# Two-block transformer kernel: down biases in one transfer over 96 partitions, the router's modulation units dealt to other places, and another order inside the first expert

## The chip, the cores and the metric

One core of a Trainium2 chip runs the whole program in one launch. The metric is the device time of an execution in microseconds (us), and the median of several executions is compared. All values are float32; the weights are read from HBM, some 585 MB in an execution.

## What is computed

Two transformer blocks run one after the other on 256 tokens of width 1024. The first has a mixer, cross attention and a mixture of experts; the second has two attention layers and two MLPs, whose modulation (`ada`) is a product of one vector with large matrices. The part that matters here is the mixture of experts (MoE):

```python
logits = (hf @ w_router) + b_router               # 256 tokens, 32 experts
top_v, top_i = lax.top_k(logits, 4)
top_w = jax.nn.softmax(top_v, axis=-1)
...
def expert_block(args):                           # for each expert e and its tokens xb
    xb, e = args
    gu = xb @ w_gate_up[e] + b_gate_up[e]         # 1024 -> 2048
    gate = jnp.minimum(gu[:, :D_EXPERT], SWIGLU_LIMIT)
    up = jnp.clip(gu[:, D_EXPERT:], -SWIGLU_LIMIT, SWIGLU_LIMIT)
    glu = gate * jax.nn.sigmoid(SWIGLU_ALPHA * gate)
    return ((up + 1.0) * glu) @ w_down[e] + b_down[e]
...
m = jax.nn.silu(c) @ w + b                        # the second block's modulation ("ada")
```

## The kernel before

The program is written engine by engine, each engine's instructions in the order in which they stand in the code, with semaphores between them. TensorE (PE) multiplies, ScalarE (ACT) and VectorE (DVE) work on what it leaves in the PSUM banks, GpSimd (POOL) does little, and SyncE (SP) issues nearly all DMAs on one queue.

**Weights in granules.** SP brings the weights in pieces of 2 MB, the granules, into eight slots of SBUF (`ring`). `PRE` is the list of granules used ahead of the experts, `FILL_ORDER` the order in which SP issues them. `SLOTS` slots are reused: a fill waits until PE has used the granule that had the slot before (semaphore `granules_used`, in the code `used`, which counts granules in the order of their use). Four granules of the modulation, `SIDE`, lie outside the ring, in free parts of `arena` and `XN`. An expert has six granules: four of `w_gate_up` (j = 0 to 3) and two of `w_down`. For the first expert these are called q0 to q5 here, and q6, q7 are the first two of the second expert. `AHEAD` says behind which granule of the modulation SP issues q0 to q5. q6 and q7 take the two ring slots in which the last two ring units of the modulation lay, so their fills wait for the use of those.

**The router's three units.** PE multiplies the modulation vector with twelve units of `ada` weights, (`ada(n)`: the next n units; line 1406). Units 9, 10 and 11 are used in the router's stage: unit 9 behind the transposes of the normalised tokens, unit 10 behind the router's logits, unit 11 behind the positions of the tokens. Before the change unit 9 is the side unit (in `arena[0:4096]`) and units 10 and 11 lie in the ring. The gate and up bias rows `bias_gu_r` are written by ACT (line 992) over a part of the same `arena` region, so ACT waits for the use of the side unit first. Behind them ACT copies the last group of the modulation (`ada_copy`, line 887) and the down biases into `dn_r` (line 996); DVE then makes the low parts (lines 2539 and 2545).

**Down biases.** `b_down` (32 experts x 1024) is wanted three times, one below the other, in 96 partitions of `dn_raw`. SP issues it between q4 and q5, in three transfers of 32 partitions.

**Small transfers at the start.** ACT issues thirteen DMAs on its own queue before it computes: six vectors of 8 rows of 512 B (`norm_mem`, `norm_mix`, `norm_xattn`, `norm_ffn`, `c_2`, `norm_final`), two of 4 rows, one of 2, one of 12, two of 24 and one of 96, 214 rows together.

**The first expert.** PE gathers its tokens (`gather`, line 1581), sends the overflow count and the transposed gates (lines 1602 and 1605; DVE makes tables and `gatT_r` from them), and waits for the gathered tokens `xe`, which DVE scales (line 2494, semaphore `e_xe`). Then come the bias rows (`bias_gu`, line 1627), four times `gate_up` (line 1635), between them `ada_combine` (line 1418), `extra_table` (lines 1612 to 1614), `down_bias` (line 1622), then the hidden layer's transposes (line 1647) and `down` (line 1654). The other 31 experts have the same form, without the tables, and with `scatter` (line 1665).

Of the kernel before, what the change touches and what calls it, by code (L numbers as in the profile page):

```python
# [19 lines left out]
F32 = mybir.dt.float32  # L20
# [7 lines left out]
P = 128  # L28
S = 256
TB = S // P  # L30
D = 1024
KC = D // P
NE = 32
# [3 lines left out]
NCAND = (NB_MAX - 1) * NE  # L37
NX_MAX = S * TOPK // CAP
SLOT = 4096
# [81 lines left out]
PRE = pre_stream()  # L121
# [4 lines left out]
SLOTS = 8  # L126
R0 = 4
R1 = 8
SIDE = {PRE.index(("ada", u)): SLOTS + i for i, u in enumerate((4, 5, 8, 9))}
SIDE_FILL = {4: 32, 5: 48, 8: 80, 9: 96}  # L130
RING = [g for g in range(NPRE) if g not in SIDE]
NR = len(RING)
assert PRE[RING[NR - R0]] == ("w_o", 0)
E_SLOTS = [7, 6, (NR - R0) % R0, (NR - R0 + 1) % R0, 4, 5] + [(NR - R0 + j) % R0 for j in range(2, R0)]
E_BLOCK = 4
HEAD = [("w_k", 0), ("w_k", 1)]
TAIL = [("w_o", 0), ("w_o", 1), ("ada", 8), ("ada", 10), ("ada", 11), ("ada", 9)]
FILL_ORDER = ([PRE.index(p) for p in HEAD] + [g for g in range(NPRE) if PRE[g] not in HEAD + TAIL]
              + [PRE.index(p) for p in TAIL])
assert len(set(FILL_ORDER)) == NPRE  # L140
AHEAD = {("ada", 8): (0,), ("ada", 11): (1,), ("ada", 9): (2, 3, 4, 5)}
SPLIT = [p for p in PRE if p[0] != "ada"]
PER_E = 6
MOE_END = NPRE + NE * PER_E
# [94 lines left out]
def build_program(nc, A, tab_d, dft_d, out_d):  # L239
    ctx = ExitStack()  # L240
    with ctx:
        sems = {}

        def sem(name):
            if name not in sems:
                sems[name] = ctx.enter_context(nc.semaphore(name))
            return sems[name]

        def done(name, i):

            if (name, i) in PRE:
                return sem("granules_used"), USED_AT[PRE.index((name, i))]
            return sem("granules_used"), MOE_END + POST.index((name, i)) + 1
# [25 lines left out]
        B = [ctx.enter_context(nc.psum_tensor(f"bank{i}", [P, HW], F32)) for i in range(8)]  # L279
# [24 lines left out]
        flag = stat[0:NCAND, 56:57]  # L304
# [6 lines left out]
        ident, tri, ones, quads, iota = (tb_(n) for n in ("ident", "tri", "ones", "quads", "iota"))  # L311
        eps5, eps6, zero = tb_("eps5"), tb_("eps6"), tb_("zero")

        def slot(s, w=SLOT):
            assert s < SLOTS
            return ring[:, s * SLOT:s * SLOT + w]

        def arn(a, w):
            return arena[:, a:a + w]
# [39 lines left out]
        dn_raw = arn(5120, D)[0:3 * NE]  # L359
        dn_r = XT_rf[0:3 * NE, 0:D]  # L360
        gatT_r = XT_rf[0:3 * NE, D:D + TB * P].rearrange("p (t n) -> p t n", t=TB)
        gat3_r = XT_rf[:, D + TB * P:D + TB * P + TB * 96].rearrange("p (t a e) -> p t a e", t=TB, a=3)
# [80 lines left out]
        def unit_parts(u):  # L443

            if u == 8:
                places = [XNf, arn(6144, 2048)]
            elif u in SIDE_FILL:
                places = [{4: slot(SLOTS - 1), 5: arn(2048, SLOT), 9: arn(0, SLOT)}[u]]
            else:
                places = [slot(slot_of(PRE.index(("ada", u))))]  # L450
            k = KC // len(places)
            return [(k * i, x.rearrange("p (k n) -> p k n", k=k)) for i, x in enumerate(places)]
# [148 lines left out]
        def _(sp):  # L601
# [8 lines left out]
            def fill(g, name, i):  # L610
                o = OWNER[g]
                if o is not None and PRE[o] in SPLIT:
                    sp.wait_ge(sem("w_hi"), half_no(PRE[o][0], 2 * PRE[o][1] + 1))
                    sp.wait_ge(sem("w_lo"), half_no(PRE[o][0], 2 * PRE[o][1] + 1))
                elif o is not None:
                    sp.wait_ge(used, USED_AT[o])
                if (name, i) == ("ada", 4):
                    sp.wait_ge(sem("fft_seq"), 4)
                elif (name, i) == ("ada", 5):
                    sp.wait_ge(sem("mix_sum"), 2)  # L620
                    sp.wait_ge(*done("ada", 4))
                elif (name, i) == ("ada", 8):
                    sp.wait_ge(*upto("xa", "sq", 2))
                    sp.wait_ge(*done("ada", 5))
                elif (name, i) == ("ada", 9):
                    sp.wait_ge(sem("xa_o"), 4)
                    sp.wait_ge(*done("ada", 8))
                for dst, src in granule_source(name, i, slot_of(g)):
                    sp.dma_start(dst, src).then_inc(landed[slot_of(g)], 16)
# [8 lines left out]

            def down_bias_fill():

                for r in range(3):
                    sp.dma_start(dn_raw[NE * r:NE * r + NE], A["b_down"][0]).then_inc(sem("bias_landed"), 16)

            def expert_source(j, e):
                if j < 4:
# [9 lines left out]
            for g in FILL_ORDER[2:]:  # L655
                name, i = PRE[g]
# [50 lines left out]
            with sp.If(n > 0):  # L707
                sp.wait_ge(used, MOE_END)
                with sp.Fori(0, n) as i:
                    e = nc.values_load(table_i[0:1, bass.ds(i, 1)], engines=[ENG.SP], min_val=0, max_val=NE - 1)  # L710
# [133 lines left out]
        def _(act):  # L844
# [142 lines left out]
                act.activation(rt[:, t, 0:NE], logit[:, t, 0:NE], ACT.Exp,  # L987
                               bias=att[:, 2, t:t + 1]).then_inc(sem("rt_e"), 1)
            act.wait_ge(sem("bias_landed"), 16 * 8)
            act.wait_ge(*done("ada", 9))  # L990
            for m in range(2):
                act.activation(bias_gu_r[m], bias_raw[m], ACT.Copy).then_inc(sem("bias_hi"), 1)
            ada_copy()
            act.wait_ge(sem("logits"), 1)
            act.wait_ge(sem("bias_landed"), 16 * 11)
            act.activation(dn_r, dn_raw, ACT.Copy).then_inc(sem("bias_hi"), 1)

            def expert(i, down_done):
# [279 lines left out]
        def _(pe):  # L1278
# [132 lines left out]
            def ada_combine():  # L1411

                a, b, _, comb = ADA_GROUPS[group[0]]
                n = b - a
                group[0] += 1
                pe.wait_ge(sem("ada_part"), group[0])
                for c in range(4):
                    mm = pe.matmul(B[comb][:, n * c:n * c + n], ada_part[:, c * P:(c + 1) * P], quads[:, 0:n],
                                   start=True, stop=True)
                mm.then_inc(sem("ada_comb"), 1)  # L1420
# [55 lines left out]
            for i, b in enumerate((6, 7, 2, 3)):  # L1476
                if b == 2:
                    pe.wait_ge(sem("mix_c"), 2)
                for e in range(TB):
                    mm = pe.matmul(B[b][:, e * S:(e + 1) * S], U[:, e, i * P:(i + 1) * P], dft[:, e * S:(e + 1) * S],  # L1480
                                   start=True, stop=True)
# [45 lines left out]
            for m in range(2):  # L1527
                for t in range(TB):
                    mm = pe.matmul(B[3][:, 2 * m + t:2 * m + t + 1], ssum[:, m, t * P:(t + 1) * P], ones[:, 0:1],
                                   start=True, stop=True)  # L1530
# [67 lines left out]
            pe.wait_ge(*upto("ffn", "xn", 2))  # L1598
            pe.wait_ge(sem("e_sel"), 2)
            gather()  # L1600
            pe.wait_ge(sem("overflow"), 1)
            pe.matmul(B[2][0:NCAND, 65:66], tri[0:NCAND, 0:NCAND], flag, start=True, stop=True).then_inc(sem("rt_mm"), 1)
            pe.wait_ge(sem("gat3"), 2)
            for t in range(TB):
                mm = pe.transpose(B[6][0:3 * NE, t * P:(t + 1) * P],
                                  gat3_r[:, t].rearrange("p a e -> p (a e)").bitcast(F32), ident)
            mm.then_inc(sem("rt_mm"), 1)

            def extra_table():

                pe.wait_ge(sem("overflow"), 2)
                pe.matmul(B[2][0:1, 96:112], tb_("cand_e")[0:NCAND, :], chosen, start=True, stop=True)
                pe.matmul(B[2][0:1, 112:128], tb_("cand_q")[0:NCAND, :], chosen, start=True, stop=True)
                pe.matmul(B[2][0:1, 128:129], ones[0:NCAND, 0:1], flag, start=True, stop=True).then_inc(sem("rt_mm"), 1)
# [10 lines left out]
            def bias_gu():  # L1625
                for m in range(2):
                    pe.matmul(B[m][:], selG, bias_gu_r[m], start=True, stop=False, skip_group_check=True)  # L1627
# [41 lines left out]
            def expert(i, n, first=False):  # L1669

                pe.wait_ge(sem("e_selG"), i * E_BLOCK + (n + 1))
                pe.wait_ge(sem("e_xe"), i * E_BLOCK + (n + 1))
                bias_gu()
                for j in range(4):
                    g = NPRE + n * PER_E + j
                    pe.wait_ge(landed[slot_of(g)], i * (16 * E_BLOCK * PER_E // R1) + FILL[g])
                    gate_up(j, slot_of(g)).then_inc(used, 1)
                    if first and j == 0:
                        ada_combine()
                        extra_table()  # L1680
                    elif first and j == 2:
                        down_bias()
                    elif j == 0:
                        pe.wait_ge(sem("e_y"), i * E_BLOCK + (n + 1))
                        pe.wait_ge(sem("e_ylo"), i * E_BLOCK + (n + 1))
                        scatter()
                pe.wait_ge(sem("e_sel"), i * (2 * E_BLOCK) + (2 * n + 4))
                gather(0, KC - 1)
                pe.wait_ge(sem("e_h"), i * E_BLOCK + (n + 1))
                hidden_T()  # L1690
                gather(KC - 1)
                pe.wait_ge(sem("e_wsel"), i * (2 * E_BLOCK) + (2 * n + 2))
                pe.wait_ge(sem("e_clamp"), i * (2 * E_BLOCK) + (2 * n + 2))
                weights_T()
                pe.wait_ge(sem("e_hTe"), i * E_BLOCK + (n + 1))
                if first:
                    pe.wait_ge(sem("table_ready"), 1)
                for j in range(2):
                    g = NPRE + n * PER_E + 4 + j
                    pe.wait_ge(landed[slot_of(g)], i * (16 * E_BLOCK * PER_E // R1) + FILL[g])  # L1700
                    down(j, slot_of(g)).then_inc(used, 1)
                pe.wait_ge(sem("e_wTe"), i * (2 * E_BLOCK) + (2 * n + 2))
# [1296 lines left out]
```

## Time and profile before

| what | value |
|---|---|
| median of three executions | 1796.16 us |
| lowest and highest of the three | 1792.27 and 1941.92 us |
| the profiled execution's own time | 1793.1 us |
| its span, first to last instruction | 1791.3 us |
| share of the span in which PE is busy | 96% |
| mean DMA rate over the span | 328 GB/s |
| granted clock of PE | 0.995 of full speed |

The profile is one execution with a record of every instruction and DMA packet. Its own time stands 1.8 us above its span, and the two lowest times of the three executions are 3.9 us apart; so terms of a microsecond are compared by the profile, not by the times.

### The profile page before, as it was taken

To read this page: it belongs to the slowest core of one execution; us is meant where nothing else is said; L and a number is where in the kernel's file an instruction comes from. 1 tells how busy PE (TensorE), PEld (TensorE's weight loads), DVE (VectorE), ACT (ScalarE), POOL (GpSimd) and SP (SyncE) were. 2 spreads that over 40 slices of the span, in tenths; PEclk is the share of its full clock that TensorE was granted. 3 is DMA by queue.
4 is the path that set the end of the run, shared out by engine and by line. 5 is a ranking of instruction groups with operands and counts; after the bars stand their busy time and mean duration, and the time that the engine had idled before them with its cause. 6 is when DMAs were issued, how large, how long until landed. Compare 5 with 4: busy or idle time off the path is not lost.

```text
span 1791.3 us, 24226 instructions
## 1 busy us (share of the span) xinstructions
PE 1724.1 (96%) x9828; PEld 1083.8 (61%) x9828; DVE 777.9 (43%) x1327; ACT 524.1 (29%) x694; POOL 33.8 (2%) x40
## 2 busy tenths in 40 slices
PE   8999999999999999999999999999999999899997
PEld 7878754443443434343434343375799988689986
DVE  4454442221221212121212121289887779676555
ACT  5353421111111111111101010247544455644442
POOL 0002000000000000000000000000000010000001
PEclk9999999999999999999999999998999999999999
DMA  9757999999999999999999999975387754335550
GB/s 347 285 200 289 371 396 429 428 427 427 428 429 428 429 428 428 429 428 429 428 428 429 428 429 428 421 283 201 118 286 269 278 205 177 124 119 188 187 210 24
DMA packets 97287, 587.54 MB, mean 328 GB/s; under 512 B 7822, under 2 KB 8036, under 8 KB 71620
## 3 DMA queue, kind: packets, MB, share of 16 engines
q1 hardware_dynamic: 95744, 582.28, 80.5%
q10 hardware_dynamic: 1476, 4.30, 0.7%
q8 instruction: 50, 0.82, 0.2%
q14 instruction: 17, 0.14, 0.0%
HBM read 585.51 MB, written 1.05 MB: 327 GB/s over the span
## 4 chain that ended last, share of the span: by engine, by line
PE 73%; DMA 20%; DVE 3%; ACT 3%; issue 1%; SPq 0%; DVEq 0%; ACTq 0%
PE bank L1321 32%; DMA ring<-in_w_gate_up 19%; PE bank L1635 15%; PE bank L1654 9%; PE bank L1581 4%; PE bank L1903 3%; PE bank L1665 1%; PE bank L1949 1%; PE bank L1627 1%; PE bank L1406 1%; ACT arena L1003 1%; PE bank L1647 1%; ACT sb_XN L1122 1%; DMA ring<-in_w_k 1%; PE bank L2160 0%
## 5 line engine op out<-in xcount | busy, mean ns | idle before, releaser
L1635 PE MATMUL bank<-ring,arena 128*64 128x512 f32 x2048 | 462.6, 597 | 29.0 <-DMA ring<-in_w_gate_up 28.8
L1635 PEld LDWEIGHTS bank<-ring,arena 128*64 128x64 f32 x2048 | 137.5, 136 | 320.2 <-issue 255.3
L1654 PE MATMUL bank<-ring,arena 128*64 128x512 f32 x1024 | 226.8, 595 | 3.3
L1321 PE MATMUL bank<-w_hi,arena_r 128*128 128x512 f32 x672 | 217.2, 392 | 0.9 <-DVE arena_r L2791 0.9
L572 DVE TENSOR_TENSOR w_lo<-ring,w_hi 128x4096 fp32r<-128x4096 f32 (+2 forms) x43 | 188.0, 4373 | 27.9 <-ACT w_hi L561 26.3
L2498 DVE TENSOR_SCALAR arena<-bank 128x512 f32<-128x512 f32 x32 | 22.1, 692 | 367.6 <-PE bank L1635 367.6
L1001 ACT ACTIVATE arena<-arena,sb_tab 128x512 f32<-128x512 f32 x32 | 23.1, 722 | 508.8 <-DVE arena L2498 508.8
L561 ACT ACTIVATE w_hi<-ring 128x4096 fp32r<-128x4096 f32 (+2 forms) x43 | 152.4, 3586 | 20.4 <-DMA ring<-in_c_w_in 12.4
L1654 PEld LDWEIGHTS bank<-ring,arena 128*64 128x64 f32 x1024 | 71.7, 137 | 137.8 <-issue 132.3
L1321 PEld LDWEIGHTS bank<-w_hi,arena_r 128*128 128x128 f32 x672 | 126.2, 188 | 29.3 <-issue 1.9
L1581 PEld LDWEIGHTS bank<-arena,sb_XN 128*128 128x128 f32 x1056 | 123.2, 192 | 26.9 <-issue 26.9
L1581 PE MATMUL bank<-arena,sb_XN 128*128 128x64 f32 x1056 | 128.4, 275 | 0.0
L1321 PE MATMUL bank<-XT_r,w_hi 128*128 128x256 f32 x448 | 127.2, 284 | 0.0
L1321 PE MATMUL bank<-arena_r,w_hi 128*128 128x256 f32 x448 | 126.8, 283 | 0.0
L1321 PE MATMUL bank<-XT_r,w_lo 128*128 128x256 f32 x448 | 126.8, 283 | 0.0
L1321 PE MATMUL bank<-w_lo,arena_r 128*128 128x512 f32 x304 | 118.5, 390 | 0.0
L2519 DVE SCALAR_TENSOR_TENSOR arena_r<-bank,sb_att,arena_r 128x512 fp32r<-128x512 f32 x32 | 24.0, 750 | 217.3 <-ACT arena_r L1006 217.3
L1006 ACT ACTIVATE arena_r<-bank,sb_att 128x512 fp32r<-128x512 f32 x32 | 22.0, 688 | 231.0 <-PE bank L1654 231.0
L545 DVE TENSOR_TENSOR half_lo<-ring,half_hi 128x2048 fp32r<-128x2048 f32 x26 | 59.5, 2290 | 67.8 <-ACT half_hi L535 67.8
L1321 PEld LDWEIGHTS bank<-XT_r,w_hi 128*128 128x128 f32 x448 | 86.0, 192 | 0.7 <-issue 0.2
L1321 PEld LDWEIGHTS bank<-arena_r,w_hi 128*128 128x128 f32 x448 | 86.0, 192 | 0.7 <-issue 0.2
L1321 PEld LDWEIGHTS bank<-XT_r,w_lo 128*128 128x128 f32 x448 | 86.0, 192 | 0.0
(427 smaller groups left out, 2187.9 us busy)
## 6 DMA issues: line engine op xcount, KB each, us to landing
ring<-in_w_gate_up SPq DMA_DIRECT2D x128, 2048.0 KB, 32.0
ring<-in_w_down SPq DMA_DIRECT2D x64, 2048.0 KB, 35.3
ring<-in_mlp_w SPq DMA_DIRECT2D x32, 2048.0 KB, 8.7
ring<-in_ada_w SPq DMA_DIRECT2D x15, 2048.0 KB, 13.3
arena<-in_ada_w SPq DMA_DIRECT2D x48, 256.0 KB, 5.5
ring<-in_c_w_in SPq DMA_DIRECT2D x6, 2048.0 KB, 8.2
ring<-in_w_in SPq DMA_DIRECT2D x4, 2048.0 KB, 8.3
ring<-in_w_v SPq DMA_DIRECT2D x2, 2048.0 KB, 24.2
```

The source lines that it names most:

```text
L545: eng.tensor_tensor(lo[:], half_raw(name, h)[1], hi[:].bitcast(F32), ALU.subtract).then_inc(sem("w_lo"), 1)
L561: ins = eng.activation(dst, raw, ACT.Copy) if on_act else eng.tensor_copy(dst, raw)
L572: eng.tensor_tensor(lo[:, 0:w], slot(slot_of(granule_no(name, i)), w), hi[:, 0:w].bitcast(F32), ALU.subtract).then_inc(sem("w_lo"), 1)
L1001: act.activation(sig, gcl, ACT.Sigmoid, bias=zero, scale=1.702).then_inc(sem("e_sig"), 1)
L1006: act.activation(y_hi, B[2][:], ACT.Copy, scale=slot_gate).then_inc(sem("e_y"), 1)
L1321: mm = pe.matmul(out, st[a], mv[b], start=start and a + b == 0, stop=stop and a == 1, skip_group_check=True)
L1581: mm = pe.matmul(B[3][:, k * CAP:(k + 1) * CAP], XN[:, t, k * P:(k + 1) * P], sel_tok[:, t, :], start=(t == 0), stop=(t == 1))
L1635: mm = pe.matmul(B[m][CAP * h:CAP * h + CAP, :], xe[:, 2 * j + kl, :], w[:, kl, m * D + h * HW:m * D + (h + 1) * HW], start=False, stop=(j ...
L1654: mm = pe.matmul(B[2][CAP * h:CAP * h + CAP, :], hT[:, c, CAP * j:CAP * j + CAP], w[:, c, h * HW:(h + 1) * HW], start=(j == 0 and c == 0), ...
L1903: mm = pe.matmul(b, x[:, k, t * P:(t + 1) * P], parts[wa][:, kl, width * c:width * c + width], start=k + xa + wa == 0, stop=False, skip_gr ...
L2498: dve.tensor_scalar(gcl, B[0][:], 7.0, None, ALU.min).then_inc(sem("e_clamp"), 1)
L2519: dve.scalar_tensor_tensor(y_lo, B[2][:], slot_gate, y_hi.bitcast(F32), ALU.mult, ALU.subtract).then_inc(sem("e_ylo"), 1)
```

## The change

Three things are changed. The down biases come in one transfer whose source names `b_down` three times by a step of 0, over 96 partitions. Of the router's three units, 9 and 10 now lie in the ring and 11 is the side unit. In every expert `bias_gu` now stands ahead of the wait for the tokens. In the first expert the overflow count and the gate transposes (`gates_T`) come behind the first granule, and `extra_table` behind the second.

```diff
-SIDE = {PRE.index(("ada", u)): SLOTS + i for i, u in enumerate((4, 5, 8, 9))}
+SIDE = {PRE.index(("ada", u)): SLOTS + i for i, u in enumerate((4, 5, 8, 11))}
-TAIL = [("w_o", 0), ("w_o", 1), ("ada", 8), ("ada", 10), ("ada", 11), ("ada", 9)]
+TAIL = [("w_o", 0), ("w_o", 1), ("ada", 8), ("ada", 9), ("ada", 10), ("ada", 11)]
-AHEAD = {("ada", 8): (0,), ("ada", 11): (1,), ("ada", 9): (2, 3, 4, 5)}
+AHEAD = {("ada", 8): (0,), ("ada", 10): (1,), ("ada", 11): (2, 3, 4, 5)}
...
-                for r in range(3):
-                    sp.dma_start(dn_raw[NE * r:NE * r + NE], A["b_down"][0]).then_inc(sem("bias_landed"), 16)
+                sp.dma_start(dn_raw, A["b_down"][0][None].to_broadcast((3, NE, D))).then_inc(sem("bias_landed"), 16)
...
             act.wait_ge(sem("bias_landed"), 16 * 8)
-            act.wait_ge(*done("ada", 9))
+            act.wait_ge(*done("ada", 11))
             for m in range(2):
                 act.activation(bias_gu_r[m], bias_raw[m], ACT.Copy).then_inc(sem("bias_hi"), 1)
             ada_copy()
             act.wait_ge(sem("logits"), 1)
-            act.wait_ge(sem("bias_landed"), 16 * 11)
+            act.wait_ge(sem("bias_landed"), 16 * 9)
...
-            pe.wait_ge(sem("overflow"), 1)
-            pe.matmul(B[2][0:NCAND, 65:66], tri[0:NCAND, 0:NCAND], flag, start=True, stop=True).then_inc(sem("rt_mm"), 1)
-            pe.wait_ge(sem("gat3"), 2)
-            for t in range(TB):
-                mm = pe.transpose(B[6][0:3 * NE, t * P:(t + 1) * P],
-                                  gat3_r[:, t].rearrange("p a e -> p (a e)").bitcast(F32), ident)
-            mm.then_inc(sem("rt_mm"), 1)
+            def gates_T():
+
+                pe.wait_ge(sem("overflow"), 1)
+                pe.matmul(B[2][0:NCAND, 65:66], tri[0:NCAND, 0:NCAND], flag, start=True, stop=True).then_inc(sem("rt_mm"), 1)
+                pe.wait_ge(sem("gat3"), 2)
+                for t in range(TB):
+                    mm = pe.transpose(B[6][0:3 * NE, t * P:(t + 1) * P],
+                                      gat3_r[:, t].rearrange("p a e -> p (a e)").bitcast(F32), ident)
+                mm.then_inc(sem("rt_mm"), 1)
...
                 pe.wait_ge(sem("e_selG"), i * E_BLOCK + (n + 1))
+                bias_gu()
                 pe.wait_ge(sem("e_xe"), i * E_BLOCK + (n + 1))
-                bias_gu()
...
                     if first and j == 0:
+                        gates_T()
                         ada_combine()
+                    elif first and j == 1:
                         extra_table()
```

On PE, between the logits and the positions of the tokens, the units stand like this before (`slot0` and `slot1` are ring slots, `arena` the side place):

```order
L1406 MATMUL bank<-ring,sb_cs 32x512 [waits slot0_landed]
L1406 MATMUL bank<-ring,sb_cs 32x512 x7
L1312 MATMUL bank<-sb_tab 128x128 x2
L1591 MATMUL bank<-sb_rt,sb_tab 128x32 [waits rt_mask]
L1592 MATMUL bank<-sb_rt,sb_tab 128x32
L1593 MATMUL bank<-sb_rt,sb_tab 128x32
L1595 MATMUL bank<-sb_tab,sb_vec 96x1 x2
L1406 MATMUL bank<-ring,sb_cs 32x512 [waits slot1_landed]
```

and like this in the changed kernel:

```order
L1405 MATMUL bank<-ring,sb_cs 32x512 [waits slot1_landed]
L1405 MATMUL bank<-ring,sb_cs 32x512 x7
L1311 MATMUL bank<-sb_tab 128x128 x2
L1590 MATMUL bank<-sb_rt,sb_tab 128x32 [waits rt_mask]
L1591 MATMUL bank<-sb_rt,sb_tab 128x32
L1592 MATMUL bank<-sb_rt,sb_tab 128x32
L1594 MATMUL bank<-sb_tab,sb_vec 96x1 x2
L1405 MATMUL bank<-arena,sb_cs 32x512 [waits arena_landed]
```

The ring slots are used by units 9 and 10 in place of 10 and 11, and the side place by the last unit in place of the first.

On PE, from the gather of the first expert's tokens to its second granule (`slot7` has q0, `slot6` has q1), before:

```order
L1581 MATMUL bank<-arena,sb_XN 128x64 x15
L1602 MATMUL bank<-sb_stat,sb_tab 96x1 [waits overflow]
L1605 MATMUL bank<-sb_tab,XT_r 96x128 [waits gat3]
L1605 MATMUL bank<-sb_tab,XT_r 96x128
L1627 MATMUL bank<-arena_r 128x512 [waits e_selG,e_xe,bias_lo,ada_part]
L1627 MATMUL bank<-arena_r 128x512
L1635 MATMUL bank<-ring,arena 64x512 [waits slot7_landed]
L1635 MATMUL bank<-ring,arena 64x512 x7
L1418 MATMUL bank<-sb_tab,arena 128x3 [waits ada_part]
L1418 MATMUL bank<-sb_tab,arena 128x3 x3
L1612 MATMUL bank<-sb_stat,sb_tab 1x16 [waits overflow]
```

and in the changed kernel:

```order
L1580 MATMUL bank<-arena,sb_XN 128x64 x15
L1629 MATMUL bank<-arena_r 128x512 [waits e_selG,bias_lo,ada_part]
L1629 MATMUL bank<-arena_r 128x512
L1637 MATMUL bank<-ring,arena 64x512 [waits slot7_landed,e_xe]
L1637 MATMUL bank<-ring,arena 64x512 x7
L1604 MATMUL bank<-sb_stat,sb_tab 96x1 [waits overflow]
L1607 MATMUL bank<-sb_tab,XT_r 96x128 [waits gat3]
L1607 MATMUL bank<-sb_tab,XT_r 96x128
L1417 MATMUL bank<-sb_tab,arena 128x3 [waits ada_part]
L1417 MATMUL bank<-sb_tab,arena 128x3 x3
L1637 MATMUL bank<-ring,arena 64x512 [waits slot6_landed]
```

The wait for the tokens (`e_xe`) now stands at the first granule and no longer at the bias rows; three short matmuls moved behind the first granule, and the three of line 1612 to 1614 behind the second.

On SP's queue, around the down biases, before:

```order
L653 DMA ring<-in_w_gate_up 128x4096 [waits w_lo,w_hi] x2
L653 DMA ring<-in_w_down 128x4096 [waits granules_used]
L642 DMA arena<-in_b_down 32x1024 [waits granules_used]
L642 DMA arena<-in_b_down 32x1024 x2
L653 DMA ring<-in_w_down 128x4096
L653 DMA ring<-in_w_gate_up 128x4096 [waits granules_used] x4
```

and in the changed kernel:

```order
L652 DMA ring<-in_w_gate_up 128x4096 [waits w_lo,w_hi] x2
L652 DMA ring<-in_w_down 128x4096 [waits granules_used]
L641 DMA arena<-in_b_down 96x1x1024 [waits granules_used]
L652 DMA ring<-in_w_down 128x4096
L652 DMA ring<-in_w_gate_up 128x4096 [waits granules_used] x4
```

Three issues became one. Its destination has 96 rows of 4 KB; its source is written as 3 copies (step 0) of 32 rows of 4 KB.

## Rows read from the trace of the kernel before

**Rows 1.** The page: its head, and shares of the chain that ended last

```profile
span 1791.3 us, 24226 instructions
...
PE 73%; DMA 20%; DVE 3%; ACT 3%; issue 1%; SPq 0%; DVEq 0%; ACTq 0%
```

**Rows 2.** The chain that ended last, 566 to 650 us: start, us, what

```profile
579.91 34.15 DMA ring<-in_w_gate_up
614.10 3.65 PE bank L1635 x16
...
638.50 34.29 DMA ring<-in_w_gate_up
```

**Rows 3.** The same chain, 250 to 300 us

```profile
257.07 3.27 PE bank L1581 x28
...
261.60 7.09 PE bank L1654 x32
...
289.04 7.09 PE bank L1654 x32
```

**Rows 4.** The same chain, 1085 to 1160 us: the last expert

```profile
1142.66 3.65 PE bank L1635 x16
```

**Rows 5.** Windows: us, busy time (x instructions) of each engine, clock, DMA share, GB/s

```profile
225.00:228.00 3.00, 3.00 (x38) 1.19 (x36) 2.24 (x6) 2.98 (x8) 1.46 (x11) 1.00 0.82 300
228.00:231.00 3.00, 3.00 (x32) 1.46 (x24) 2.06 (x12) 0.65 (x1) 0.00 (x0) 1.00 0.99 388
231.00:234.00 3.00, 2.88 (x26) 1.89 (x26) 2.64 (x14) 1.57 (x4) 0.00 (x0) 1.00 1.07 253
234.00:237.00 3.00, 2.97 (x29) 2.01 (x21) 2.65 (x16) 1.64 (x2) 0.00 (x0) 1.00 0.97 367
...
250.00:575.00 325.00, 323.85 (x1706) 141.09 (x1702) 69.67 (x151) 39.50 (x48) 0.00 (x0) 1.00 1.01 428
```

**Rows 6.** Timeline of SP's queue, 220 to 250 us

```profile
224.11 1.75 SPq L642 DMA_DIRECT2D arena<-in_b_down  x3
...
231.39 17.90 SPq L653 DMA_DIRECT2D ring<-in_w_gate_up  x4
```

**Rows 7.** Timeline of PE, 222 to 246 us

```profile
225.51 1.92 PE L1406 MATMUL bank<-arena,sb_cs 128*32 128x512 f32 x16
...
235.15 3.76 PE L1581 MATMUL bank<-arena,sb_XN 128*128 128x64 f32 x32
238.74 0.28 PE L1602 MATMUL bank<-sb_stat,sb_tab 96*96 96x1 f32 x2
238.88 0.40 PE L1605 MATMUL bank<-sb_tab,XT_r 128*96 128x128 f32 x2
239.85 0.70 PE L1627 MATMUL bank<-arena_r 128*128 128x512 f32 x2 [0.57 <-DVE arena L2494]
240.48 3.65 PE L1635 MATMUL bank<-ring,arena 128*64 128x512 f32 x16
```

**Rows 8.** Timeline of ACT, 215 to 265 us

```profile
231.69 1.13 ACT L992 ACTIVATE arena_r<-arena 128x512 fp32r<-128x512 f32 x2
235.19 0.60 ACT L887 ACTIVATE arena<-bank 128x512 f32<-128x512 f32 x1 [2.37 <-PE bank L1406]
235.96 1.06 ACT L996 ACTIVATE XT_r<-arena 96x1024 fp32r<-96x1024 f32 x1 [0.17 <-DMA arena<-in_b_down]
```

**Rows 9.** Timeline of DVE, 218 to 262 us

```profile
237.47 1.29 DVE L2539 TENSOR_TENSOR arena_r<-arena,arena_r 64x512 fp32r<-64x512 f32 x2
...
239.74 1.22 DVE L2545 TENSOR_TENSOR XT_r<-arena,XT_r 32x1024 fp32r<-32x1024 f32 x1
...
245.38 0.18 DVE L2555 CAST sb_table_i<-bank 1x33 int32<-1x33 f32 x1 [3.11 <-PE bank L1614]
```

**Rows 10.** DMA view, 0 to 14 us: ACT's queue (packets, MB, share of 16 engines)

```profile
q10 hardware_dynamic: 324, 0.11, 3.2%
```

**Rows 11.** DMA view, 1170 to 1180 us: busy tenths in 40 slices

```profile
DMA  9999999999977776453222100000000000000000
```

More of the change, by code:

```diff
@@ L128 @@
 R1 = 8
-SIDE = {PRE.index(("ada", u)): SLOTS + i for i, u in enumerate((4, 5, 8, 9))}
-SIDE_FILL = {4: 32, 5: 48, 8: 80, 9: 96}
+SIDE = {PRE.index(("ada", u)): SLOTS + i for i, u in enumerate((4, 5, 8, 11))}
+SIDE_FILL = {4: 32, 5: 48, 8: 80, 11: 96}
 RING = [g for g in range(NPRE) if g not in SIDE]
@@ L447, in unit_parts @@
             elif u in SIDE_FILL:
-                places = [{4: slot(SLOTS - 1), 5: arn(2048, SLOT), 9: arn(0, SLOT)}[u]]
+                places = [{4: slot(SLOTS - 1), 5: arn(2048, SLOT), 11: arn(0, SLOT)}[u]]
             else:
@@ L624, in fill @@
                     sp.wait_ge(*done("ada", 5))
-                elif (name, i) == ("ada", 9):
+                elif (name, i) == ("ada", 11):
                     sp.wait_ge(sem("xa_o"), 4)
```

## The prediction

> **What bounds the kernel now.** I read the page's head first: PE is busy nearly everywhere, and the chain that ended last is PE for 73% and DMA for 20% of the span [rows 1]. The chain itself says where the DMA part lies. From about 580 us on it reads: granule issued, 34 us in the queue, landed at 614.06, then PE's `gate_up` on it, then the next such wait [rows 2]. Two experts take 638.50 - 579.91 = 58.6 us there, 29.3 us each. Before that stretch an expert takes 289.04 - 261.60 = 27.4 us and PE waits for no granule [rows 3]: the eight slots were full when the experts began, and PE eats 29.3 - 27.4 = 1.9 us of this lead with each expert, some twelve times until 580 us: a lead of about 20 us. But the DMA engines move 428 GB/s with a busy share of 1.01 from 250 to 575 us [rows 5], so they are full in the PE-bound stretch too. From about 230 us to the last expert's last `gate_up` at 1142.66 [rows 4] the end is therefore set by one quantity: how much time the slowest of the 16 DMA engines spends on anything but moving granules back to back. A microsecond that PE gains or loses near 240 us only changes the lead; a microsecond that the DMA engines lose stays to the end.
>
> **The profiled execution as base.** Its time is 1793.1 us, between the lowest (1792.27) and the median (1796.16) of the three. I make the sum against 1793.1.
>
> **Part 1, the first expert's order on PE.** Before, PE ends the gather at 235.15 + 3.76 = 238.91, sends the flag product and the gate transposes until 239.28, waits for the tokens, and runs the bias rows from 239.85 and the first granule from 240.48 [rows 7]. DVE has the low parts of the bias rows at 237.47 + 1.29 = 238.76 [rows 9], so the bias rows can now run right behind the gather, and the first granule starts about when the tokens come, 239.85: 0.7 us earlier. Behind it the flag product and transposes cost 239.28 - 238.74 = 0.5 us that were hidden in the wait. Net: PE is 0.2 us ahead, into a lead of 20 us, worth 0. DVE's table copy moves with `extra_table` from 245.38 [rows 9] behind the second granule, to about 248.7; behind it DVE must write the next selection before the gather at 257.07 [rows 3]. Cover: 8 us less those short operations; if it were gone, PE would wait into its lead. Worth 0.
>
> **Part 2, the router's units.** The side place's last user is now unit 11. ACT, which wrote the bias rows at 231.69, must wait for that unit and starts about 235.2, where its copy of the group starts today [rows 8]. Its work is then 1.13 + 0.60 us and ends near 237.0; DVE takes the first bias rows at 237.47 [rows 9] and waits for nothing. The copy of the down biases follows behind, at 237.1 instead of 235.96 [rows 8], done at 238.2, and DVE wants it at 239.74 [rows 9]. Cover 1.5 us, worth 0. On SP, q6 waits for unit 9 instead of unit 10 and issues at about 225.51 + 1.92 = 227.4 instead of 231.39 [rows 6, 7]; q7 moves likewise by 4 us. But q4 and q5 are queued ahead of them, and the DMA share is 0.99 to 1.07 from 228 to 234 us [rows 5]: the engines aren't waiting for q6. Worth 0. The fall to 300 GB/s at 225 us [rows 5] lies ahead of q4's first bytes; q4 waits for PE's output projection, which the change doesn't touch, and an earlier q6 can't pass q4, which stands ahead of it on SP. So this idle time stays.
>
> **Part 3, the down biases.** Here the stream itself is touched. Today the three transfers carry 96 x 4 KB = 0.39 MB. At 428 GB/s that is 0.9 us. The windows from 228 to 237 us show 388, 253 and 367 GB/s at full busy share [rows 5]; against 428 they are short by (40 + 175 + 61)/428 x 3 = 1.9 us. So the down biases now cost the stream about 0.9 + 1.9 = 2.8 us.
>
> What the one transfer costs depends on how its 96 rows are dealt to the engines. Another row bears on that. ACT's thirteen transfers have 214 rows and left 324 packets [rows 10]; 110 are over. Taken as one completion packet for each engine that a transfer uses, 16 engines each would give 208, and as many engines as rows up to 16 would give 118. The largest number up to 16 that divides the row count gives 6 x 8 + 4 + 4 + 2 + 12 + 12 + 12 + 16 = 110. So a transfer's engines here follow its leading dimension. The new transfer leads with 96 at its destination and with 3 copies at its source. No row shows a transfer whose two sides differ; I take 3, the number that divides both.
>
> The Trainium skill, "DMA: Bandwidth & Descriptors", section "Why a DMA increments its semaphore by 16 and not by 1", says so outright: the number of engines is the largest one up to 16 that divides the slowest dimension of both sides. Its "Rules for kernel authors" warn of exactly a leading step-0 broadcast, which confines a DMA to as many engines as it has copies. The count of 110 agrees with it; that the source's 3 decides, only the page states. It speaks against this change.
>
> With three engines each carries 32 rows, 131 KB. An engine moves 428/16 = 26.8 GB/s, so 4.9 us; at the rate of the dip, 253/16 = 15.8 GB/s [rows 5], 8.3 us. Against the 2.8 us that these engines lose today: +2.1 to +5.5 us. The engines don't end together, though. When the queue drains near 1174 us, the busy share falls from full to nothing over 3 us (12 slices of 0.25 us) [rows 11]: the slowest engine is some 3 us behind the first. If the three are early ones, up to 3 us of their extra is hidden. So the stream ends -0.9 to +5.5 us later; I take +2, the middle, since the rows don't say where the three stand.
>
> ACT's copy then waits longer, as the three engines' share lands 5 to 8 us after q4's, near 236 to 240 us in place of 235.8. Behind it are queued on ACT a table load and nothing else before the sigmoid at 258 us; on DVE its low part, the memset of `y_lo`, and the tables for `extra_table`, which PE now reaches near 248.5 us. A landing at 240 gives the copy at 241.1, the low part at 242.3 and, with three short operations behind it, the tables near 244. Cover 4 us. In the old order PE reached `extra_table` at 245, so part 1 is what hides this.
>
> **Sum.** 0 + 0 + 2 = +2 us: 1795 us.
>
> **Rivals.**
> *The extra is hidden.* The three engines are early ones, or their 4 KB rows run at full rate beside little traffic. For it: 3 us of unevenness [rows 11]. Against: all three must be early. The end moves by -0.9 to 0: 1792.6 us.
> *All sixteen engines.* The destination's 96 decides, the change does what it says: one completion for three. Up to the 1.9 us of the dip come back, less if the dip is from three copies of the same 128 KB being read and written at once, which stays: -1.9 to 0, 1792 us. For it: 96 divides by 16, as ACT's transfer of 96 rows did. Against: a source of 3 copies.
> *Slower: one engine.* If the mismatch of the two sides makes the dealing fall back to one engine, 0.39 MB take 14.7 us at 26.8 GB/s and 24.9 us at 15.8. Less today's 2.8 and up to 3 of lead: +9 to +22 us, say 1808 us. It would pass 2% (36 us) only at under 10 GB/s. PE would stay unstalled until the lead of 20 us is used, and the tables would make PE wait from a landing at about 245 us on. Against it: every leading count of those thirteen with a common divisor used more than one engine.
>
> **How the numbers follow.** Three engines and exposed 0.62; three and hidden 0.13; sixteen 0.18; one 0.04; something that I don't see 0.03. All but part of the last two lie within 2%, which is about what a measurement of this kernel can tell from no change. The likeliest case's bounds are 1793.1 to 1798.6; the medians lie up to 3 us above the profiled execution and the lowest time 0.8 below; the sixteen-engine case reaches down to 1791.2. That makes 1790 to 1802, with the one-engine case outside. Faster by over 2%: 0.01; slower by over 2%: 0.02.
>
> **What would show it.** In the changed profile: the window in which the down biases run has a lower rate than 253 GB/s, or a longer one, with a busy share that falls to that of three engines if the others run out, and 3 completion packets in place of 48; the copy of line 995 waits for the transfer by some us; PE's first granule starts near 239.9; q6 issues near 227.4; the chain's last DMA wait ends near 1144.6 instead of 1142.6. I am wrong if that wait ends earlier than 1142, or if PE waits for a granule near 260 us.

## The result, and the profile after

The changed kernel takes 1799.09 us (median of 15 executions, 1797.01 to 1801.28); the kernel before 1795.43 us in 15. One execution of before, 1941.92 us, was disturbed and is left out of the ratio, which is 1.0019 with a 95% interval of 1.0012 to 1.0026: 2.2 to 4.7 us slower, a small loss that is clear of noise. The forecast was 1795 us, in a range of 1790 to 1802. The time lies in the range, but 1795 is below both medians of before, so as a statement on the change it had the wrong sign.

The page of the changed kernel: its head, its count of packets, and the chain that ended last by engine:

```profile
span 1797.3 us, 24213 instructions
...
DMA packets 97242, 587.54 MB, mean 327 GB/s; under 512 B 7777, under 2 KB 7991, under 8 KB 71575
...
PE 70%; DMA 23%; DVE 3%; ACT 2%; issue 1%; ACTq 0%; SPq 0%; DVEq 0%
```

The same line of packets on the page of before:

```profile
DMA packets 97287, 587.54 MB, mean 328 GB/s; under 512 B 7822, under 2 KB 8036, under 8 KB 71620
```

The bytes are the same, and 45 packets under 512 B are gone. Three transfers on 16 engines have 48 completion packets, one transfer on three engines has 3: the difference is exactly 45. The chain's DMA share rose from 20% [rows 1] to 23%: PE runs into the stream's waits earlier. The chain's waits for granules begin at 469.81 and 525.14 us, where before the first is the one at 579.91 [rows 2].

Windows of the changed kernel (columns as in [rows 5]):

```profile
228.00:231.00 3.00, 3.00 (x32) 1.46 (x24) 2.07 (x12) 0.68 (x1) 0.00 (x0) 1.00 0.99 421
231.00:234.00 3.00, 2.87 (x26) 1.89 (x26) 2.64 (x14) 0.53 (x2) 0.00 (x0) 1.00 1.14 315
234.00:237.00 3.00, 2.96 (x29) 1.97 (x21) 2.65 (x16) 1.63 (x3) 0.00 (x0) 1.00 0.95 212
237.00:240.00 3.00, 2.81 (x22) 2.30 (x23) 2.35 (x5) 0.00 (x0) 0.00 (x0) 1.00 1.02 243
240.00:243.00 3.00, 3.00 (x16) 0.86 (x12) 1.14 (x1) 2.21 (x2) 0.00 (x0) 1.00 0.94 385
```

The dip is deeper and about 9 us long, where before it was one window of 253 GB/s between two milder ones [rows 5]. The busy share stays near 1: the engines without rows of `b_down` don't run dry, they are slowed as well. The trace's packet records show it directly. The granules' 16 KB packets that started from 234 to 240 us took 1.1 us in the mean, and 0.61 us from 243 to 252 us.

The first expert, timeline of PE in the changed kernel:

```profile
235.19 3.75 PE L1580 MATMUL bank<-arena,sb_XN 128*128 128x64 f32 x32
238.90 0.70 PE L1629 MATMUL bank<-arena_r 128*128 128x512 f32 x2
239.80 3.65 PE L1637 MATMUL bank<-ring,arena 128*64 128x512 f32 x16 [0.19 <-DVE arena L2498]
243.38 0.33 PE L1604 MATMUL bank<-sb_stat,sb_tab 96*96 96x1 f32 x2
...
248.27 0.20 PE L1614 MATMUL bank<-sb_stat,sb_tab 96*1 96x16 f32 x2
```

Here every time of part 1 came out: the first granule at 239.80 in place of 240.48 [rows 7], the tables' matmuls at 248.27. ACT's copy of the down biases and DVE's low part behind it:

```profile
240.78 1.06 ACT L995 ACTIVATE XT_r<-arena 96x1024 fp32r<-96x1024 f32 x1 [3.86 <-DMA arena<-in_b_down]
```

```profile
241.86 1.22 DVE L2549 TENSOR_TENSOR XT_r<-arena,XT_r 32x1024 fp32r<-32x1024 f32 x1 [2.12 <-ACT XT_r L995]
...
244.03 0.41 DVE L2557 CAST XT_r<-bank 96x256 fp32r<-96x256 f32 x1
```

ACT waited 3.86 us for the biases, where before it was 0.17 [rows 8], and the tables were ready at 244.4, 4 us before PE came. The order hid the transfer's lateness, as forecast. What it couldn't hide is in the chain that ended last, at the last expert:

```profile
1112.44 34.28 DMA ring<-in_w_gate_up
...
1146.77 3.65 PE bank L1637 x16
```

The last `gate_up` starts at 1146.77 in place of 1142.66 [rows 4]: 4.1 us of the loss were there when the experts ended. This start is the best instrument of the case and is called the **end of the stream** below. The rest of the 6 us between the two spans lies behind it (see the base, below).

### The profile page after: what moved, and what is told of

Read it like the earlier page. It is cut to its first block, busy times and chain, and to the rows that moved or that the text cites. A ratio compares the mean times of both kernels' runs of the same rounds, so it can differ in the third digit from the quotient of the medians.

```text
span 1797.3 us, 24213 instructions
## 1 busy us (share of the span) xinstructions
PE 1728.4 (96%) x9828; PEld 1085.4 (60%) x9828; DVE 778.0 (43%) x1327; ACT 524.6 (29%) x694; POOL 33.8 (2%) x40
## 3 DMA queue, kind: packets, MB, share of 16 engines
HBM read 585.51 MB, written 1.05 MB: 326 GB/s over the span
## 4 chain that ended last, share of the span: by engine, by line
PE 70%; DMA 23%; DVE 3%; ACT 2%; issue 1%; ACTq 0%; SPq 0%; DVEq 0%
PE bank L1320 32%; DMA ring<-in_w_gate_up 23%; PE bank L1637 14%; PE bank L1656 8%; PE bank L1580 4%; PE bank L1907 3%; PE bank L1953 1%; PE bank L1667 1%; PE bank L1405 1%; PE bank L1629 1%; ACT arena L1002 1%; PE bank L1649 1%; PE bank L1812 1%; PE bank L2164 0%; DMA ring<-in_ada_w 0%
```

## The experiments

Times are medians, ratios are to the kernel before on the same chip.

**transfer_only**: only the transfer is changed, the rest is the kernel before.

```diff
-                for r in range(3):
-                    sp.dma_start(dn_raw[NE * r:NE * r + NE], A["b_down"][0]).then_inc(sem("bias_landed"), 16)
+                sp.dma_start(dn_raw, A["b_down"][0][None].to_broadcast((3, NE, D))).then_inc(sem("bias_landed"), 16)
...
-            act.wait_ge(sem("bias_landed"), 16 * 11)
+            act.wait_ge(sem("bias_landed"), 16 * 9)
```

> The kernel before with only the down biases changed to the one transfer with a leading step-0 dimension of 3; PE's order and the router's units stay as before. Theory A (three engines carry the transfer and the slowest of them sets the end of the expert stream): slower than before by what the whole change costs, ratio 1.0015 to 1.0025 (+3 to +4.5 us); the last expert's last gate_up near 1146.7 us in place of 1142.7. In addition PE reaches the tables near 245 us, some 1 us before DVE has them, and waits there, which costs nothing at the end. Theory B (the new order on PE and ACT costs part of it): ratio under 1.001.

Measured: 1799.69 us, ratio 1.0027 (1.0016 to 1.0037), end of the stream 1147.53. The whole loss is there, so theory A; both numbers lie a little above what I expected. PE's wait at the tables exists and is worth nothing:

```profile
245.60 0.20 PE L1611 MATMUL bank<-sb_stat,sb_tab 96*1 96x16 f32 x2 [0.43 <-DVE sb_stat L2549]
```

**order_only**: the changed kernel with the three transfers of before, the reverse of the diff above.

> The changed kernel with the down biases in three transfers again; the rest of the change stays. Theory A: no difference from before, ratio 0.9995 to 1.0005, the last gate_up near 1142.7 us; PE's first granule starts at 239.8 us and the lead that this gives is worth nothing. Theory B: the later bias rows, tables and the earlier q6 and q7 cost 1 us or more, ratio over 1.0005.

Measured: 1794.6 us, ratio 1.0000 (0.9991 to 1.0009), end of the stream 1143.57. By the time there is no cost, which fells theory B as far as 1.6 us. The end of the stream is 0.9 us later than before's, and a second profile of before gave 1142.66 again. By what I wrote down ahead of that second profile, the 0.9 us would then be a cost of the new order. But the two profiles of the changed kernel stand 1.0 us apart, and sixteen_engines below, in the same new order, ends 0.7 us earlier than before. So a cost of up to 0.9 us to the stream is neither shown nor excluded.

**sixteen_engines**: one transfer again, but from 96 rows of their own. They are rows of another weight, so this kernel leaves the down biases out.

```diff
-                sp.dma_start(dn_raw, A["b_down"][0][None].to_broadcast((3, NE, D))).then_inc(sem("bias_landed"), 16)
+                sp.dma_start(dn_raw, A["w_o"][0][0:3 * NE, :]).then_inc(sem("bias_landed"), 16)
```

> The changed kernel with one transfer of 96 rows of 4 KB whose source has 96 rows of its own (rows of another weight in place of b_down, so the down biases are left out and other numbers stand in their place). Both sides lead with 96. Theory A: all 16 engines, 16 completion packets, the stream loses no more than before: last gate_up 1141 to 1143 us, ratio 0.999 to 1.000. If it is the merging itself that costs (one long transfer, no further engines), ratio 1.0015 or more as in the changed kernel.

Measured: 1795.15 us, ratio 0.9999 (0.9990 to 1.0008), end of the stream 1141.92. The page has 97256 packets, 31 fewer than before; in all packet records of the trace the 4 B ones are 32 fewer, which is 48 less 16. Merging three transfers into one costs nothing when it runs on all engines.

**two_engines**: 96 rows of another weight in two groups of 48, no step of 0; the down biases are left out here too.

```diff
-                sp.dma_start(dn_raw, A["b_down"][0][None].to_broadcast((3, NE, D))).then_inc(sem("bias_landed"), 16)
+                sp.dma_start(dn_raw, A["w_o"][0].rearrange("(a b) n -> a b n", a=2)[:, 0:48]).then_inc(sem("bias_landed"), 16)
```

> The changed kernel with one transfer of 96 rows of 4 KB whose source is 2 groups of 48 rows of another weight (so the down biases are left out and other numbers stand in their place); nothing in it is repeated by a step of 0. Theory A: what counts is the smaller common divisor of the two sides, whatever the step: two engines with 48 rows each, 2 completion packets; between the three engines (+4 us) and the one engine (+17 us): 48 x 0.27 = 13 us of these engines less the 2.8 us of before and 1 to 2 us that they are early, last gate_up 8 to 10 us later than before, ratio 1.004 to 1.006. Rival: the step of 0 is what hurt (three reads of the same rows at once), then this one costs nothing: ratio 0.9995 to 1.0005.

Measured: 1802.41 us, ratio 1.0045 (1.0031 to 1.0058), end of the stream 1149.79; its page has 97241 packets, 46 fewer than before, which is 48 less 2. The end is 7.1 us later than before, a little under the 8 to 10 that I expected. The repeated reading isn't needed for the loss: a source without it, dealt to two engines, is worse than the step of 0 on three. Whether the repeated reading adds a part of its own on three engines was not tried.

**one_engine**: the same 96 rows as transfers of 31 and 1 partitions.

```diff
-                sp.dma_start(dn_raw, A["b_down"][0][None].to_broadcast((3, NE, D))).then_inc(sem("bias_landed"), 16)
+                for r in range(3):
+                    sp.dma_start(dn_raw[NE * r:NE * r + NE - 1], A["b_down"][0][0:NE - 1]).then_inc(sem("bias_landed"), 16)
+                    sp.dma_start(dn_raw[NE * r + NE - 1:NE * r + NE], A["b_down"][0][NE - 1:NE]).then_inc(
+                        sem("bias_landed"), 16)
...
-            act.wait_ge(sem("bias_landed"), 16 * 9)
+            act.wait_ge(sem("bias_landed"), 16 * 14)
```

> The changed kernel with the down biases in three pairs of transfers, 31 partitions and 1 partition each: the same 96 rows of 4 KB. By theory A and the rule that the number of engines divides the leading dimension, all 96 rows run on one engine: 96 x 0.27 us = 26 us of that engine, less the 2.8 us of before and what it is early: the last gate_up 18 to 25 us later than before, ratio 1.010 to 1.014. The number of completion packets is 6 in place of 48. If the rows are dealt over the engines whatever the leading dimension is, ratio 0.999 to 1.001.

Measured: 1812.22 us, ratio 1.0096 (1.0081 to 1.0111), end of the stream 1159.47, 16.8 us later than before, a little under what I expected; 97246 packets, 41 fewer, and 42 fewer of 4 B in all packet records, which is 48 less 6. This is the slower rival of the prediction, built as a kernel, and it shows what the three-engine case hides. SP's queue was held while it issued the last two transfers, so q5 went out at 232.96 in place of 225.91:

```profile
225.75 2.38 SPq L642 DMA_DIRECT2D arena<-in_b_down  x1
228.18 4.36 SPq L643 DMA_DIRECT2D arena<-in_b_down  x1
232.96 0.47 SPq L655 DMA_DIRECT2D ring<-in_w_down  x1
```

Meanwhile the other engines ran out of work. Two windows, the second inside the first:

```profile
231.00:234.00 3.00, 2.87 (x26) 1.89 (x26) 2.64 (x14) 0.53 (x2) 0.00 (x0) 1.00 0.11 45
231.50:232.90 1.40, 1.27 (x12) 1.08 (x11) 1.33 (x6) 0.27 (x2) 0.00 (x0) 1.00 0.07 26
```

In the second window the one engine is alone, and it moves its 4 KB rows at 26 GB/s: full rate, 0.16 us each. From 237 us on, with the other engines busy again, its rows took 0.28 us each in the packet records.

And the biases landed at 253.8, so DVE's tables came at 257 and PE stood still for them (the waits of this kernel, 228 to 300 us):

```profile
PE bank L1617 <- DVE sb_stat L2557: 8.9, 1, 8.9
```

These 8.9 us of PE don't appear at the end beside the stream's 16.8: they were paid from the lead.

**no_down_load**: the transfer is left out, and with it the down biases; GpSimd writes zeros to `dn_raw`.

```diff
-                sp.dma_start(dn_raw, A["b_down"][0][None].to_broadcast((3, NE, D))).then_inc(sem("bias_landed"), 16)
...
+            pool.memset(dn_raw, 0.0).then_inc(sem("conv_pad"), 1)
...
-            act.wait_ge(sem("bias_landed"), 16 * 9)
+            act.wait_ge(sem("conv_pad"), 3)
```

> The changed kernel without the transfer of the down biases; GpSimd writes zeros in their place, so the down biases are left out of the result. This measures the whole cost of the transfer to the stream. My term: 2.8 us less than before, last gate_up near 1139.9 us, ratio 0.998 to 0.999. If the fall of the rate near 231 us is not the transfer's doing, under 1 us.

Measured: 1793.53 us, ratio 0.9991 (0.9982 to 1.0000), end of the stream 1142.38. Read alone this end would say 0.3 us. But the profiled execution was late from its first 50 us on: SP issued q4 at 225.44, where in the other profiles it is 223.7 to 223.9:

```profile
225.44 0.80 SPq L652 DMA_DIRECT2D ring<-in_w_down  x2
```

With the 1.7 us taken off, the end is 1140.7: the transfer cost 2.0 us before. That is a correction of one profile. The completion packets give a second reading nearer to the transfer: the last engine finished its part of the granule behind q7 at 253.38 us, 251.7 with the 1.7 taken off, and before at 254.79. By that the transfer cost 3.1 us before, and a later delay in that profile took 1 us of it back. So it is 2 to 3 us, where I had expected 2.8. The dip is gone from the windows:

```profile
231.00:234.00 3.00, 2.88 (x24) 1.21 (x23) 2.47 (x15) 0.53 (x2) 0.00 (x0) 1.00 1.01 431
234.00:237.00 3.00, 2.97 (x28) 1.48 (x27) 2.64 (x14) 0.05 (x1) 0.00 (x0) 1.00 1.02 437
```

**gate_up_rows_two_engines**: few engines again, at another place. The kernel before, with the 0.5 MB of `b_gate_up` rows at 158 us in four transfers with a leading 2.

```diff
-                    for r in range(4):
-                        a = m * D + HW * (r % 2)
-                        sp.dma_start(bias_raw[m][NE * r:NE * r + NE], A["b_gate_up"][0][:, a:a + HW]).then_inc(
-                            sem("bias_landed"), 16)
+                    for r in range(2):
+                        sp.dma_start(bias_raw[m][2 * NE * r:2 * NE * r + 2 * NE],
+                                     A["b_gate_up"][0][:, m * D:m * D + D].rearrange("e (h n) -> h e n", h=2)).then_inc(
+                            sem("stored"), 16)
```

> The kernel before with the rows of b_gate_up (0.5 MB at 158 us) in four transfers with a leading dimension of 2 in place of eight with 32: two engines carry 256 KB each, 10 to 17 us in place of 2 us. Behind them stand the second half of w_o (issued at 170 us) and later granules, and the DMA engines are idle at 168 to 171, 179 to 181 and near 187 us. Theory: an engine that is late only costs where the stream is full behind it; here the idle gaps take it up, at least half of it, ratio 1.000 to 1.003. If few engines cost the same everywhere: 8 to 15 us, ratio 1.0045 to 1.008.

Measured: 1793.6 us, ratio 0.9995 (0.9986 to 1.0004), end of the stream 1142.12: nothing, though each of two engines carries 256 KB, twice what each of the three carries in the changed kernel. (These transfers count on another semaphore, and the waits for it are changed with them.) Its windows:

```profile
168.00:171.00 3.00, 3.00 (x27) 3.00 (x27) 2.36 (x4) 0.00 (x0) 0.00 (x0) 1.00 0.13 51
171.00:174.00 3.00, 3.00 (x27) 3.00 (x27) 0.00 (x0) 0.00 (x0) 0.00 (x0) 1.00 0.94 255
174.00:177.00 3.00, 3.00 (x27) 3.00 (x26) 0.00 (x0) 0.00 (x0) 0.00 (x0) 1.00 1.02 278
177.00:180.00 3.00, 2.70 (x21) 1.00 (x21) 0.00 (x0) 2.72 (x5) 0.00 (x0) 1.00 0.56 210
```

At 168 us the share is 0.13, two sixteenths: the two engines alone. The next granule is then slower and runs until 180, in the time in which the kernel before had idle engines, and no wait of PE changes for it.

**one_copy**: a version meant to be faster. `b_down` comes once; ACT writes its high part twice, DVE the low part between them.

```diff
-                sp.dma_start(dn_raw, A["b_down"][0][None].to_broadcast((3, NE, D))).then_inc(sem("bias_landed"), 16)
+                sp.dma_start(dn_raw[0:NE], A["b_down"][0]).then_inc(sem("bias_landed"), 16)
...
-            act.activation(dn_r, dn_raw, ACT.Copy).then_inc(sem("bias_hi"), 1)
+            act.activation(dn_r[0:NE], dn_raw[0:NE], ACT.Copy).then_inc(sem("bias_hi"), 1)
+            act.activation(dn_r[2 * NE:3 * NE], dn_raw[0:NE], ACT.Copy).then_inc(sem("bias_hi"), 1)
...
-            link(dve.tensor_tensor(dn_r[NE:2 * NE], dn_raw[NE:2 * NE], dn_r[NE:2 * NE].bitcast(F32), ALU.subtract))
+            link(dve.tensor_tensor(dn_r[NE:2 * NE], dn_raw[0:NE], dn_r[0:NE].bitcast(F32), ALU.subtract))
...
                 pe.wait_ge(sem("gat3"), 3)
+                pe.wait_ge(sem("bias_hi"), 4)
```

> The changed kernel with b_down loaded once, into 32 partitions (2 rows for each of 16 engines); ScalarE writes its high part into the first and the third 32 partitions, VectorE the low part into the second, all three out of the one copy. Theory: of the 2.8 us that the biases cost the stream before, two thirds or more are saved: last gate_up 1140 to 1141.5 us in place of 1142.7, ratio to the kernel before 0.9983 to 0.9995. The added 1.1 us on ScalarE lies in its idle time until 257 us. If only bytes count and not the crowding, 0.6 us are saved: ratio 0.9995 to 1.

> The version with one copy of b_down again, to narrow its interval: ratio 0.9985 to 0.9998 and the interval below 1 if it beats the kernel before by 1 us or more; if it straddles 1 again at a ratio over 0.9995, it is no better than before by anything that can be told.

Measured: 1793.54 us, ratio 0.9993 (0.9984 to 1.0002), end of the stream 1141.44; the second time 1794.42 us, 0.9996 (0.9987 to 1.0005), end 1141.60. The stream ends 1.1 to 1.2 us earlier than before, in both profiles, but the times don't tell it from no change. It is faster than the changed kernel by some 5 us.

**before_again** and **after_again**: the two kernels unchanged, one more profile each, of a single execution.

> The kernel before, unchanged: a second profile, to see how far two profiles of one kernel stand apart. The last gate_up of the experts differs by up to 1 us from 1142.7; a stretch of half clock near 1550 us is there (as in the profile of the changed kernel, not in the one of before), and then the time is 1795 to 1796 us in place of 1793.1. If the profiles of one kernel agree within 0.3 us instead, the 0.9 us between before and order_only is a cost of the new order.

> The changed kernel, unchanged: a second profile. Last gate_up 1146 to 1148 us; time 1797 to 1800 us, the lower one if the stretch of half clock near 1550 us is missing. If the last gate_up lies under 1145 us, the three engines' extra varies with where they stand, and 4.1 us was one case.

Measured: 1794.1 us with the end of the stream at 1142.66, and 1800.58 us with the end at 1147.77. The first time is under the 1795 to 1796 that I expected, the second a little above its range. So two profiles of before agree at this point, and the three with the transfer on three engines lie at 1146.77, 1147.53 and 1147.77.

## Why the prediction was right and wrong

**The bound** held. In every kernel the time followed the end of the stream, and PE's gains and waits near 240 us did not: 0.7 us gained in the changed kernel, 8.9 us lost in one_engine.

**Parts 1 and 2 at 0** held by the time, within the interval of order_only (1.6 us either way) and the 0.9 us that its end of the stream leaves open. The covers named were the right ones: ACT's bias rows started at 235.28, DVE took them without a wait, and part 1's later tables hid the late biases.

**Part 3, the dealing** held: three engines, shown by 45 completion packets less, by two_engines and by sixteen_engines. The Trainium skill's rule ("DMA: Bandwidth & Descriptors", "Why a DMA increments its semaphore by 16 and not by 1") says so, and these runs agree with it at 1, 2, 3 and 16 engines.

**Part 3, the size**, +2 us, was too small: measured +4.1 and +5.1 us at the end of the stream in the two profiles, +4.9 in transfer_only. That is inside the +2.1 to +5.5 of the exposed case and outside of what I took. The term that was mis-sized is the time of the 32 rows on their engine, 4.9 to 8.3 us. In the packet records the rows of `b_down` run from 230.45 to 239.65 us in the changed kernel, 9.2 us, and 10.3 and 10.2 us in after_again and transfer_only: above the whole range. A 4 KB row took 0.27 to 0.31 us there in the mean, where I had 0.15 at the engine's rate and 0.26 at the rate of the dip. The windows went down to 212 GB/s, below the 253 from which I took the slow rate.

The other two terms held. The transfer's cost before was sized at 2.8 us and is 2 to 3 (no_down_load). And the three engines were early ones, as the hidden case has it: they start their rows at 230.45 to 230.91 us, while the last engine finished q4 at 232.64. The sum from measured terms goes 9.2 less 2 to 3 less what was hidden, and it must give 4.1, so 2 to 3 us were hidden, more than the half of 3 that I took off. In two_engines and one_engine the rows ran 12.8 and 21.9 us and the end moved by 9.1 and 18.8 against 1140.7, a number that is itself uncertain by 1 us: there too some 2 to 4 us don't show.

The bound shows here as well. On thirteen engines the granule behind q7 was complete by 255.60 us, 0.8 us later than on all sixteen before. The engine whose rows ended at 239.64 finished its next granules at 244.53, 249.44 and 254.33, so by these steps of 4.9 us it was at about 259.2 (an estimate) with the one that was complete by 254.79 before: 4.4 us later, and the end moved by 4.1. The trace doesn't name the engines; completions were matched to them by these steps alone.

**The base** gave the wrong sign. This is the step that failed in the forecast as a whole: "I make the sum against 1793.1." The profiled execution was a fast one, 3.1 us under the median of 1796.16 that stood beside it, and the 1795 was then read as a time among medians; +2 us on the median would have been 1797 to 1798. With 15 executions the median of before is 1795.43. So the mechanism was right and its direction too, and the number came out below the time of the kernel before. That 1799.09 lies inside the range is partly luck: it was reached by a larger loss than forecast on a higher base. One place where it was fast can be seen. Windows of before, before_again and the changed kernel, behind the experts, the last moved by 4 us:

```profile
1551.00:1556.00 5.00, 4.48 (x40) 3.01 (x40) 4.43 (x23) 4.97 (x21) 0.00 (x0) 1.00 0.05 20
```

```profile
1551.00:1556.00 5.00, 4.98 (x38) 3.30 (x37) 3.67 (x18) 4.94 (x20) 0.00 (x0) 0.82 0.05 18
```

```profile
1555.00:1560.00 5.00, 5.00 (x29) 3.28 (x30) 3.09 (x13) 4.52 (x18) 0.00 (x0) 0.53 0.09 36
```

The granted clock (the column ahead of the last two) was 1.00, 0.82 and 0.53 there, in the same part of the program. From the end of the stream to the end of the span it takes 1791.3 - 1142.66 = 648.6 us, 649.6 and 650.5. So of the 6.0 us between the two first profiles 4.1 are the change and 1.9 come behind the experts, where before_again shows that the kernel before has such stretches too. Over all thirteen profiles this last part takes 648.3 (two_engines, with the changed order and a late stream) to 651.1 us (one_engine), so it belongs to the scatter and not to the change; that the clock alone makes the 1.9 us was not tried.

## What to carry to other kernels

Before merging small transfers, look at the slowest dimension of both sides: a leading broadcast or group count of 3 puts the whole transfer on three DMA engines, and three transfers on sixteen are cheaper. What that costs depends on what is queued behind it: nothing ahead of an idle gap; in a stream that is full to its end, 4 to 5 us here with 32 rows of 4 KB on each of three engines, 7 us with 48 on two and 17 us with 96 on one. Size such a row by what it takes beside full traffic, here 0.25 to 0.31 us, and not by the 0.16 us that it takes alone. State a small forecast against the median of many executions, and use a point inside the trace (here the last wait on the stream) to measure it.

## What the runs showed of the hardware that was not expected

- A transfer on few engines slows the others: with three, 212 and 243 GB/s for 6 us at a busy share of about 1, where the three alone missing would leave 13/16 of 428, which is 348. 16 KB packets of the granules took 1.1 us in that time, 0.85 to 1.0 us from 231 to 240 us with two engines, 0.70 to 0.74 us from 237 to 252 us with one, and 0.61 us from 231 to 240 us without the transfer (no_down_load). Why they are slowed was not tried.
- It is mutual: a 4 KB row took 0.16 us on an engine alone (26 GB/s) and 0.28 us beside full traffic, both in one_engine.
- SP's queue can be held by transfers on one engine: two issues took 2.38 and 4.36 us, where the first two took 0.33 and 0.24 us, and a granule behind them was issued 7 us late.
- A late PE costs nothing while the stream is the bound: 8.9 us of waiting went unseen in a run whose end moved with its stream alone.
- In one_copy ScalarE and VectorE wrote to 32 partitions other than those they read, in 1.05 us and 1.22 us for 1024 elements, as fast as in place (1.04 and 1.22 us).
